# Two late weight transfers of a mixture-of-experts layer, each cut into 112, 8 and 8 partitions

## The chip, the cores and the metric

The kernel runs on one core of one Trainium2 chip. The metric is the device time of one execution in microseconds (us); shorter is better. The profile comes from one further execution that the hardware profiler recorded. PE is TensorE, ACT is ScalarE, DVE is VectorE, POOL is GpSimd, and SP is SyncE, which here only issues DMAs. SP's own instructions are marked SPq, and PE's weight loads PEld.

## What is computed

One layer of a decoder with 256 tokens of width 1024: two attention mixers, then a sparse feed-forward part with 32 experts of which each token takes four, then a norm. All the time this document speaks of lies in the experts:

```python
def moe_ffn(x, w_router, b_router, w_gate_up, b_gate_up, w_down, b_down):
    ...
    def expert_step(acc, params):
        wgu, bgu, wd, bd, g = params
        hgu = xt @ wgu + bgu
        gate = jnp.minimum(hgu[:, :D_EXPERT], SWIGLU_LIMIT)
        up = jnp.clip(hgu[:, D_EXPERT:], -SWIGLU_LIMIT, SWIGLU_LIMIT)
        y = ((up + 1.0) * (gate * jax.nn.sigmoid(SWIGLU_ALPHA * gate))) @ wd + bd
        return acc + g[:, None].astype(y.dtype) * y, None
    ...
return rmsnorm(h, norm_final_g)
```

Per expert the float32 weights are 8 MB for gate and up and 4 MB for down, 12 MB in all, and 32 experts make 384 MB that have to come in from memory.

## The kernel before

Each expert's weights come through a ring of ten slots in the on-chip memory, `ring`, each slot 128 partitions by 16 KB, so 2 MB. Four slots (0 to 3, or 4 to 7, in turn) hold an expert's gate and up weights, and slots 8 and 9 (`DN0` and `DN0 + 1`) hold the two halves of its down weights. SP issues every weight transfer, in one queue, in an order written out by hand (`experts` in the sync block). Before each transfer it waits on a counter of PE (`gu_used` or `dn_used`) that tells that the slot is free. Each slot has a semaphore (`slot_in`) that a transfer raises by 16 when all of it has landed, and PE waits on that before it reads the slot.

The experts are numbered 0 to 31 (`E - 1` is the last). PE works one expert apart: while it multiplies the gate and up weights of expert g (`gate_up`, line 1893), it does the down product of expert g - 1 (`down_rows`, line 1933). Between them it transposes the hidden values (`hidden_columns`, lines 1921 to 1925), which ACT copies back (line 913) as the left operand of the down product.

The end is written out by itself. SP issues, as the last of its queue: the second half of the down weights of expert 30 into slot 9 (line 534, through line 437), then `last_down`: the first half of the down weights of expert 31 into slot 0 (line 480), which has long been used, and the second half into slot 1 as one transfer of 1 MB (line 481) and two of 512 KB (line 484). After them comes the row of final gains (`gfin`, line 546). PE's `last_expert` waits for slot 9 at line 1999, does three of its four parts, transposes the hidden values of expert 31, and does the fourth part (line 2002). Then `last_down` waits for the copy by ACT (line 1960) and for slot 0 (line 1961), and does the last down product out of slots 0 and 1. `last_scatters` adds the result to the output banks, and DVE and ACT do the final norm.

A transfer of one slot, and PE's wait for it, are these lines:

```python
def load_dn(e, q):
    sp.dma_start(ring[:, DN0 + q, :], rows_of(dn, e, q)).then_inc(slot_in[DN0 + q], 16)
...
def down_rows(s, place, js, ready, uses, columns=hT, to=6):
    pe.wait_ge(ready, uses * 16)
```

Each of the 128 partitions of such a transfer takes one row of 16 KB that lies in one piece in memory. The program has a second copy of the expert code for further passes over more tokens (`more_passes`); it is branched over here.

Of the kernel before, what the change touches and what calls it, by code (L numbers as in the profile page):

```python
# [46 lines left out]
def hybrid_layer(nc, x, norm_mix_g, w_in, w_proj_sb, w_proj_moba, w_out, rel_bias, norm_ffn_g,  # L47
# [10 lines left out]
    E = w_router.shape[2]  # L58
# [4 lines left out]
    DN = 2  # L63
    DN0 = 2 * GU
    RING = DN0 + DN
    SLOT = 4 * D
    TURN = 6
    MIXED = 3
    CH = 512
    NCH = w_in.shape[2] // CH  # L70
    TRI = 3 * P
    assert NT == 2 and KD == 8 and HSB == 8 and HMB == 8 and NCH == 10 and E == 32 and CH == HALF

# [21 lines left out]
    with ctx:  # L95
        def sb(name, shape, dt=F32):
            return ctx.enter_context(nc.sbuf_tensor(name, shape, dt))

        def sem(name):
            return ctx.enter_context(nc.semaphore(name))  # L100
# [8 lines left out]
        ring = sb("ring", [P, RING, SLOT])  # L109
# [20 lines left out]
        neg_tri = sb("neg_tri", [P, P])  # L130
        neg_one = ring[:, 5, 7 * CH:7 * CH + P]
        before = sb("before", [P, P], BF16)
# [27 lines left out]
        gatesT = gates[:, :, :].rearrange("p t d -> p (t d)").rearrange("p (g n) -> p g n", n=T)  # L160
        gate_t = gates[:, 0, 0:CH]
        sig_t = gates[:, 0, CH:2 * CH]
        up_t = gates[:, 0, 2 * CH:3 * CH]
        h_t = gates[:, 0, 3 * CH:4 * CH]
# [10 lines left out]
        hT_last = gate_t.rearrange("p (c s) -> p c s", c=4)  # L175
# [95 lines left out]
        merged_rd = sem("merged_rd")  # L271
        slot_in = [sem(f"slot_in{s}") for s in range(RING)]
        half_in = sem("half_in")
        half_used = sem("half_used")
        spare_in = sem("spare_in")
        extra_in = sem("extra_in")
        gfin_in = sem("gfin_in")
        last_in = [sem(f"last_in{q}") for q in range(4)]
# [62 lines left out]
        dn_used = sem("dn_used")  # L341
# [39 lines left out]
        def _(sp):  # L381
# [42 lines left out]
            dn = w_down[0].rearrange("e (s p r) n -> e s p (r n)", p=P, r=4)  # L424

            def rows_of(src, e, q):
                return src[e, q] if isinstance(e, int) else src[bass.ds(e, 1), q].rearrange("o p n -> p (o n)")
# [8 lines left out]
            def load_dn(e, q):  # L436
                sp.dma_start(ring[:, DN0 + q, :], rows_of(dn, e, q)).then_inc(slot_in[DN0 + q], 16)
# [34 lines left out]
            def load_down(e, done, qs=range(DN)):  # L472
                for q in qs:
                    sp.wait_ge(dn_used, (e + done) * DN + (q + 1 - DN))
                    load_dn(e, q)

            def last_down(done):

                sp.wait_ge(gu_used, (E - 2 + done) * GU + DN)
                sp.dma_start(ring[:, 0, :], dn[E - 1, 0]).then_inc(last_in[0], 16)  # L480
                sp.dma_start(ring[:, 1, 0:2 * D], dn[E - 1, 1][:, 0:2 * D]).then_inc(last_in[1], 16)
                sp.wait_ge(gu_used, (E - 2 + done) * GU + DN + 1)
                for j in (2, 3):
                    sp.dma_start(ring[:, 1, j * D:(j + 1) * D], dn[E - 1, 1][:, j * D:(j + 1) * D]).then_inc(last_in[j], 16)

            def experts(done):
                if isinstance(done, int):
                    sp.wait_ge(start_rd, 2 * NT)
                    sp.dma_start(down_one[0], dn[1, 0][:, 0:2 * D]).then_inc(spare_in, 16)
                    sp.wait_ge(half_used, 1)  # L490
                    sp.dma_start(ring[:, 0, 0:2 * D], rows_of(gu, 2, 0)[:, 0:2 * D]).then_inc(half_in, 16)
                    sp.wait_ge(gu_used, 1)
                    sp.dma_start(ring[:, 0, 2 * D:4 * D], rows_of(gu, 2, 0)[:, 2 * D:4 * D]).then_inc(slot_in[0], 16)
                    load_gate_up(2, 0, done, range(1, GU))
                    load_gate_up(3, GU, done)
                    load_down(1, done, range(1, DN))
                    sp.wait_ge(dn_used, 1)
                    load_dn(2, 0)
                else:
                    load_gate_up(2, 0, done)  # L500
                    load_gate_up(3, GU, done)
                    load_down(1, done)
                load_gate_up(4, 0, done)
                load_down(2, done, range(1, DN) if isinstance(done, int) else range(DN))
                load_gate_up(5, GU, done)
                load_down(3, done)
                load_gate_up(6, 0, done)
                load_down(4, done)
                with sp.Fori(2, TURN) as i:
                    load_gate_up_wide(i * 2 + 3, GU, done)  # L510
                    load_down(i * 2 + 1, done)
                    load_gate_up_wide(i * 2 + 4, 0, done)
                    load_down(i * 2 + 2, done)
                with sp.Fori(TURN, TURN + MIXED) as i:
                    load_gate_up_wide(i * 2 + 3, GU, done, range(0, 1))
                    load_down(i * 2 + 1, done)
                    load_gate_up_wide(i * 2 + 3, GU, done, range(1, 2))
                    load_gate_up_wide(i * 2 + 4, 0, done, range(0, 1))
                    load_down(i * 2 + 2, done)
                    load_gate_up_wide(i * 2 + 4, 0, done, range(1, 2))  # L520
                with sp.Fori(TURN + MIXED, E // 2 - 3) as i:
                    load_down(i * 2 + 1, done)
                    load_gate_up_wide(i * 2 + 3, GU, done)
                    load_down(i * 2 + 2, done)
                    load_gate_up_wide(i * 2 + 4, 0, done)
                load_down(E - 5, done)
                load_gate_up(E - 3, GU, done)
                load_down(E - 4, done)
                load_gate_up(E - 2, 0, done)
                load_down(E - 3, done)  # L530
                load_gate_up(E - 1, GU, done, range(0, 2))
                load_down(E - 2, done, range(0, 1))
                load_gate_up(E - 1, GU, done, range(2, GU))
                load_down(E - 2, done, range(1, DN))
                last_down(done)

            def another_pass(r):
# [970 lines left out]
        def _(pe):  # L1508
# [418 lines left out]
            def down_rows(s, place, js, ready, uses, columns=hT, to=6):  # L1927
                pe.wait_ge(ready, uses * 16)
                for j in js:
                    k = 4 * s + j  # L1930
                    rows = columns[:, j, SLOTS * s:SLOTS * s + SLOTS]
                    for c in range(2):
                        ins = mm(bank[to][SLOTS * c:SLOTS * (c + 1), :], rows,  # L1933
                                 ring[:, place, j * D + c * CH:j * D + (c + 1) * CH], start=k == 0, stop=k == KD - 1)
                return ins
# [22 lines left out]

            def last_down(g, uses):
                pe.wait_ge(hT_rd, g + 1)  # L1960
                down_rows(0, 0, range(4), last_in[0], uses, hT_last, 5).then_inc(dn_used, 1)
                down_rows(1, 1, range(0, 2), last_in[1], uses, hT_last, 5)
                down_rows(1, 1, range(2, 3), last_in[2], uses, hT_last, 5)
                down_rows(1, 1, range(3, 4), last_in[3], uses, hT_last, 5).then_inc(dn_used, 1)
# [19 lines left out]
                else:  # L1984
                    down(g - 1, dn_uses, fewer=fewer)

            def last_expert(g, gu_uses, dn_uses, odd):

                gate_up(g, (0, 1), GU, gu_uses, odd)
                scatter_rows(g - 2)  # L1990
                weight_columns(g - 1)
                gate_up(g, (2, 3), GU, gu_uses, odd)
                pe.wait_ge(gT_rd, g)
                hidden_columns(g - 1)
                pe.wait_ge(y_rd, g - 1)
                down(g - 1, dn_uses, range(0, 1))
                gate_up(g, (4, 5, 6, 7), GU, gu_uses, odd)
                weight_columns(g)
                down_rows(1, DN0 + 1, range(0, 3), slot_in[DN0 + 1], dn_uses)
                pe.wait_ge(gT_rd, g + 1)  # L2000
                hidden_columns(g)
                down_rows(1, DN0 + 1, range(3, 4), slot_in[DN0 + 1], dn_uses).then_inc(dn_used, 1)
# [7 lines left out]
            def experts(done, r):  # L2010
                passes = 0 if r is None else r
                gu_before, dn_before = passes * (E // 2), passes * (E - 1)
# [35 lines left out]
                    expert(i * 2 + (done + 2), True, True, 0, i + (gu_before + 2), i * 2 + (dn_before + 2))  # L2048
                expert(done + (E - 3), True, True, GU, gu_before + E // 2 - 1, dn_before + (E - 3), 5 * passes + 4)
                expert(done + (E - 2), True, True, 0, gu_before + E // 2, dn_before + (E - 2), 5 * passes + 5)  # L2050
                last_expert(done + (E - 1), gu_before + E // 2, dn_before + (E - 1), 5 * passes + 5)
                last_down(done + (E - 1), passes + 1)
                last_scatters(done + (E - 1))

# [23 lines left out]
```

## Time and profile before

| what | us |
|---|---|
| median of 3 runs | 1134.36 (1134.32 to 1134.42) |
| profiled execution, its own time | 1135.26 |
| its span, first to last instruction | 1133.5 |
| PE busy | 1073.5 (95% of the span) |
| DVE, ACT, POOL busy | 260.1, 151.2, 122.1 |
| moved by DMA | 437.30 MB, mean 386 GB/s |

The span is what the profile shows in detail; 1135.26 less 1133.5, so 1.76 us, lies around it. "Idle before" an instruction is the time in which its engine did nothing, with what ended it. The DMA share of a stretch is the mean busy share of the core's 16 DMA engines. A matmul with float32 operands stands in the trace as two records; their durations overlap, so a group's start and total are used here, not its sum.

### The profile page before, as it was taken

Reading aid. Unit: us, or ns where it says so; the run is one execution under the profiler, and the core shown is the slowest. Engines: PE = TensorE matmul, PEld = TensorE weight load, DVE = VectorE, ACT = ScalarE, POOL = GpSimd, SP = SyncE. Lnnn points to the kernel's source line nnn. Section 1 sums busy time; section 2 is a strip of 40 time slices with the busy share of each in tenths; the row PEclk is TensorE's granted clock in tenths of the full one; section 3 lists DMA queues with packets and bytes.
Section 4 is the critical chain, followed back from the end, with each engine's and each line's share of the span. In section 5 each row is a group of like instructions: output and inputs, shape, how many; then the busy total and the mean of one; then the engine's idle time right before and its main releaser. Section 6 shows DMA issues by size and latency. Waiting matters only on the chain.

```text
span 1133.5 us, 14439 instructions
## 1 busy us (share of the span) xinstructions
PE 1073.5 (95%) x6022; PEld 452.1 (40%) x6022; DVE 260.1 (23%) x482; ACT 151.2 (13%) x315; POOL 122.1 (11%) x140
## 2 busy tenths in 40 slices
PE   8999999999999999999999999999999999999986
PEld 7676444533334333333333333333333333333322
DVE  2346756621111122111111122111210101111112
ACT  2233222420000010000000010000000000001002
POOL 1357592400000000000000000000000000000000
PEclk9999999999999999999999999999999999999999
DMA  9943238899999999999999999999999999999995
GB/s 326 350 175 149 95 137 352 348 379 426 430 427 432 430 426 430 431 428 430 431 429 436 429 434 430 430 430 432 430 429 435 429 429 431 431 427 427 427 427 227
DMA packets 36273, 437.30 MB, mean 386 GB/s; under 512 B 4440, under 2 KB 5520, under 8 KB 16944
## 3 DMA queue, kind: packets, MB, share of 16 engines
q1 hardware_dynamic: 34320, 435.44, 91.3%
q10 hardware_dynamic: 1920, 1.39, 0.5%
q8 instruction: 24, 0.39, 0.1%
q14 instruction: 9, 0.07, 0.0%
HBM read 435.76 MB, written 1.06 MB: 385 GB/s over the span
## 4 chain that ended last, share of the span: by engine, by line
PE 58%; DMA 38%; DVE 2%; issue 1%; ACT 0%; SPq 0%; POOL 0%; POOLq 0%
DMA ring<-in_w_down_dram 27%; PE bank L1893 20%; PE bank L1933 13%; DMA ring<-in_w_gate_up_dram 11%; PE bank L1572 9%; PE bank L1556 5%; PE bank L1868 3%; PE bank L1861 2%; PE bank L1924 1%; PE bank L1656 1%; PE bank L1881 1%; PE bank L1918 0%; PE bank L1681 0%; PE bank L1516 0%; PE bank L2007 0%
## 5 line engine op out<-in xcount | busy, mean ns | idle before, releaser
L1893 PE MATMUL bank<-ring,gates 128*64 128x512 f32 x2048 | 472.9, 604 | 16.8 <-DMA ring<-in_w_gate_up_dram 16.7
L1933 PE MATMUL bank<-ring,gates 128*64 128x512 f32 x1008 | 225.2, 594 | 27.8 <-DMA ring<-in_w_down_dram 27.0
L1893 PEld LDWEIGHTS bank<-ring,gates 128*64 128x64 f32 x2048 | 139.2, 138 | 262.9 <-issue 231.2
L1404 DVE TENSOR_SCALAR gates<-bank 128x512 f32<-128x512 f32 x31 | 21.4, 692 | 714.1 <-PE bank L1893 714.1
L1933 PEld LDWEIGHTS bank<-ring,gates 128*64 128x64 f32 x1008 | 71.7, 137 | 175.8 <-issue 139.4
L698 POOL COPY expert_sel<-expert_row 96x64 bf16 x32 | 7.5, 234 | 843.5 <-PE bank L1861 837.9
L608 POOL TENSOR_TENSOR ring<-ring 128x512 f32<-128x512 f32 x60 | 82.4, 1408 | 66.7 <-DVE ring L1061 34.6
L1861 PEld LDWEIGHTS bank<-onehot,qkT 128*128 128x128 bf16 x1488 | 52.1, 118 | 25.2 <-issue 25.2
L1868 PE MATMUL bank<-gates,scatter_w 64*128 64x512 f32 x248 | 61.8, 615 | 0.0
L918 ACT ACTIVATE gates<-gates 128x512 f32<-128x512 f32 x32 | 20.2, 630 | 284.2 <-DVE gates L1404 284.0
L1861 PE MATMUL bank<-onehot,qkT 128*128 128x64 bf16 x1488 | 55.5, 198 | 0.0
L1572 PE MATMUL bank<-ring 128*128 128x512 f32 x112 | 51.0, 597 | 1.1 <-DVE gates L1098 1.0
L922 ACT ACTIVATE gates<-bank 128x512 f32<-128x512 f32 x32 | 19.1, 597 | 203.0 <-PE bank L1933 203.0
L1572 PE MATMUL bank<-ring,extra 128*128 128x512 f32 x96 | 42.7, 595 | 0.0
L1868 PEld LDWEIGHTS bank<-gates,scatter_w 64*128 64x128 f32 x248 | 21.3, 186 | 39.8 <-issue 39.8
L913 ACT ACTIVATE gates<-bank 128x512 f32<-128x512 f32 x32 | 19.1, 597 | 120.4 <-PE bank L1924 120.4
L907 ACT ACTIVATE stat<-stat 128x1 f32<-128x1 f32 x32 | 6.5, 202 | 197.6 <-PE bank L1918 197.6
L1572 PEld LDWEIGHTS bank<-ring 128*128 128x128 f32 x112 | 20.7, 190 | 26.4 <-issue 23.0
L1556 PE MATMUL bank<-qkT,ring 128*128 128x256 f32 x128 | 29.0, 387 | 0.0
L1556 PE MATMUL bank<-ring 128*128 128x256 f32 x128 | 28.4, 381 | 0.0
L1924 PEld LDWEIGHTS bank<-ident,gates 128*128 128x128 f32 x128 | 17.9, 209 | 26.0 <-issue 26.0
L1572 PEld LDWEIGHTS bank<-ring,extra 128*128 128x128 f32 x96 | 18.0, 190 | 22.5 <-issue 22.5
(257 smaller groups left out, 646.9 us busy)
## 6 DMA issues: line engine op xcount, KB each, us to landing
ring<-in_w_gate_up_dram SPq DMA_DIRECT2D x44, 4096.0 KB, 28.1
ring<-in_w_down_dram SPq DMA_DIRECT2D x62, 2048.0 KB, 21.1
ring<-in_w_gate_up_dram SPq DMA_DIRECT2D x39, 2048.0 KB, 14.2
ring<-in_w_in_dram SPq DMA_DIRECT2D x9, 2048.0 KB, 15.2
ring<-in_w_out_dram SPq DMA_DIRECT2D x2, 2048.0 KB, 8.7
ring<-in_w_in_dram SPq DMA_DIRECT2D x4, 512.0 KB, 7.1
ring<-in_w_proj_sb_dram SPq DMA_DIRECT2D x1, 2048.0 KB, 7.7
ring<-in_w_proj_moba_dram SPq DMA_DIRECT2D x1, 2048.0 KB, 12.6
```

The costliest lines, as they stand in the source:

```text
L608: ins = nc.gpsimd.tensor_tensor(to[:, k, :], x[:, k, :], y[:, k, :], ALU.subtract)
L913: nc.scalar.activation(to[:, :, :], bank[7][:, :].rearrange("p (c s) -> p c s", c=4), ACT.Copy).then_inc(hT_rd, 1)
L918: nc.scalar.activation(sig_t, gate_t, ACT.Sigmoid, scale=SWIGLU_ALPHA).then_inc(sig_rd, 1)
L922: nc.scalar.activation(to, bank[at][:, :], ACT.Copy).then_inc(y_rd, 1)
L1404: V.tensor_scalar(gate_t, bank[4][:, :], SWIGLU_LIMIT, None, ALU.min).then_inc(gate_rd, 1)
L1556: ins = mm(bank[(u + (u >= KD)) % 2][:, 0:T], w[:, k, j * P:(j + 1) * P], cols[:, k, :], start=k == 0, stop=k == KD - 1)
L1572: ins = mm(bank[at][:, :], a[:, t, :], b[:, t, :], start=fresh and t == 0, stop=t == n - 1, skip_group_check=not fresh)
L1861: ins = mm(bank[7][:, k * SLOTS:(k + 1) * SLOTS], pieces[i][:, t, 4 * P * (k // 4) + k % 4:4 * P * (k // 4 + 1):4], onehot[:, t, :], start ...
L1868: ins = mm(bank[2 * t + c][:, :], weights[r, t, :], y[r, :], start=False, stop=True, skip_group_check=True)
L1893: ins = mm(bank[4 + i][SLOTS * c:SLOTS * (c + 1), :], xe[:, k, :], ring[:, base + k // 2, n0:n0 + CH], start=False, stop=k == KD - 1)
L1924: ins = tp(bank[7][:, c * P:(c + 1) * P], h_t[:, c::4], ident[:, :])
L1933: ins = mm(bank[to][SLOTS * c:SLOTS * (c + 1), :], rows, ring[:, place, j * D + c * CH:j * D + (c + 1) * CH], start=k == 0, stop=k == KD - 1)
```

## The change

Two transfers of 128 partitions, the second half of expert 30's down weights (slot 9) and the first half of expert 31's (slot 0), are each issued as three: partitions 0 to 111, 112 to 119, and 120 to 127. They stand at the same places of SP's queue, in this order. For slot 9 the first piece raises `slot_in[9]` and the two small ones a new semaphore `rest_in`; PE waits for both. For slot 0 all three raise `last_in[0]`, and PE waits for 48 instead of 16. The wait of SP ahead of slot 9 is the one that `load_down` had. Nothing else is different: the same bytes go to the same places, and PE's matmuls are the same.

```diff
+    BANDS = ((0, 112), (112, 120), (120, 128))
...
+        rest_in = sem("rest_in")
...
                 sp.wait_ge(gu_used, (E - 2 + done) * GU + DN)
-                sp.dma_start(ring[:, 0, :], dn[E - 1, 0]).then_inc(last_in[0], 16)
+                for a, b in BANDS:
+                    sp.dma_start(ring[a:b, 0, :], dn[E - 1, 0][a:b]).then_inc(last_in[0], 16)
...
-                load_down(E - 2, done, range(1, DN))
+                sp.wait_ge(dn_used, (E - 2 + done) * DN)
+                for n, (a, b) in enumerate(BANDS):
+                    sp.dma_start(ring[a:b, DN0 + 1, :], dn[E - 2, 1][a:b]).then_inc(slot_in[DN0 + 1] if n == 0 else rest_in, 16)
...
-                down_rows(0, 0, range(4), last_in[0], uses, hT_last, 5).then_inc(dn_used, 1)
+                down_rows(0, 0, range(4), last_in[0], len(BANDS) * uses, hT_last, 5).then_inc(dn_used, 1)
...
-                down_rows(1, DN0 + 1, range(0, 3), slot_in[DN0 + 1], dn_uses)
+                pe.wait_ge(slot_in[DN0 + 1], dn_uses * 16)
+                down_rows(1, DN0 + 1, range(0, 3), rest_in, (len(BANDS) - 1) * uses)
```

## Rows read from the trace of the kernel before

**Rows 1.** The page's part 4: the chain that ended last, shares by engine.

```profile
PE 58%; DMA 38%; DVE 2%; issue 1%; ACT 0%; SPq 0%; POOL 0%; POOLq 0%
```

**Rows 2.** The same chain in order of time, its end: start us, us, what.

```profile
1084.39 30.19 DMA ring<-in_w_down_dram
...
1114.71 7.09 PE bank L1933 x32
1121.80 3.66 PE bank L1868 x16
```

**Rows 3.** Timeline of PE: start us, us, operation, [idle before, what ended it].

```profile
1109.69 2.79 PE L1933 MATMUL bank<-ring,gates 128*64 128x512 f32 x12 [0.87 <-DMA ring<-in_w_down_dram]
1112.42 0.75 PE L1924 MATMUL bank<-ident,gates 128*128 128x128 f32 x4
1113.10 1.08 PE L1933 MATMUL bank<-ring,gates 128*64 128x512 f32 x4
1114.71 7.09 PE L1933 MATMUL bank<-ring,gates 128*64 128x512 f32 x32 [0.53 <-DMA ring<-in_w_down_dram]
```

**Rows 4.** Timeline of DVE and ACT in the same stretch.

```profile
1110.61 0.69 DVE L1414 SCALAR_TENSOR_TENSOR gates<-gates 128x512 f32<-128x512 f32 x1
...
1113.21 0.60 ACT L913 ACTIVATE gates<-bank 128x512 f32<-128x512 f32 x1 [2.99 <-PE bank L1924]
```

**Rows 5.** Timeline of SP's issues near the end: start us, us, line.

```profile
1084.02 0.33 SPq L437 DMA_DIRECT2D ring<-in_w_down_dram  x1
1084.39 0.43 SPq L480 DMA_DIRECT2D ring<-in_w_down_dram  x1
...
1092.73 0.34 SPq L546 DMA_DIRECT2D ring<-in_norm_final_g_dram  x1
```

**Rows 6.** Line 397, the store of an 8-partition tile: how long its issue took (ns).

```profile
L397 SPq DMA_DIRECT2D u_scratch<-ring x1: 3602/3602/3602, 30.4 to 30.4; - x1
```

**Rows 7.** DMA issues from 1060 us on: KB each, median us from issue to landing.

```profile
ring<-in_w_down_dram SPq DMA_DIRECT2D x1, 1024.0 KB, 32.2
ring<-in_w_down_dram SPq DMA_DIRECT2D x2, 512.0 KB, 33.3
...
ring<-in_norm_final_g_dram SPq DMA_DIRECT2D x1, 512.0 KB, 28.0
```

**Rows 8.** Windows at the end: stretch, us, busy times, clock, DMA share, GB/s.

```profile
1115.00:1116.00 1.00, 1.00 (x6) 0.34 (x4) 0.00 (x0) 0.00 (x0) 0.00 (x0) 1.00 1.00 397
1116.00:1117.00 1.00, 1.00 (x8) 0.46 (x6) 0.00 (x0) 0.00 (x0) 0.00 (x0) 1.00 0.80 324
1117.00:1118.00 1.00, 1.00 (x8) 0.40 (x6) 0.00 (x0) 0.00 (x0) 0.00 (x0) 1.00 0.58 238
1118.00:1119.00 1.00, 1.00 (x6) 0.34 (x4) 0.00 (x0) 0.00 (x0) 0.00 (x0) 1.00 0.49 201
1119.00:1120.00 1.00, 1.00 (x8) 0.46 (x6) 0.00 (x0) 0.00 (x0) 0.00 (x0) 1.00 0.28 115
1120.00:1121.00 1.00, 1.00 (x8) 0.40 (x6) 0.00 (x0) 0.00 (x0) 0.00 (x0) 1.00 0.03 12
```

**Rows 9.** Windows in three stretches with full queues.

```profile
16.50:20.50 4.00, 4.00 (x20) 3.04 (x18) 2.84 (x3) 0.00 (x0) 0.00 (x0) 1.00 1.01 235
30.00:42.00 12.00, 12.00 (x55) 9.11 (x54) 6.63 (x7) 2.15 (x3) 3.05 (x3) 1.00 1.05 386
1041.00:1108.00 67.00, 61.03 (x360) 22.05 (x356) 9.11 (x17) 4.60 (x10) 0.47 (x2) 1.00 1.01 428
```

**Rows 10.** Line 743, three loads of 256 KB into 32 partitions each: issues, then landing.

```profile
L743 ACTq DMA_DIRECT2D gates<-in_b_gate_up_dram x3: 318/440/442, 12.5 to 13.3; - x3
...
DMA to landing us min/median/max: 6.2/7.1/7.9
```

**Rows 11.** Windows around a stretch in which PE waited: busy PE first, clock third last.

```profile
853.10:856.54 3.44, 0.92 (x6) 0.35 (x8) 0.00 (x0) 0.00 (x0) 0.00 (x0) 1.00 1.04 448
856.55:859.95 3.40, 3.40 (x12) 0.96 (x10) 0.00 (x0) 0.00 (x0) 0.00 (x0) 0.50 0.92 395
```

More of the change, by code:

```diff
@@ L1985, in expert, with last_expert @@
                     down(g - 1, dn_uses, fewer=fewer)
-            def last_expert(g, gu_uses, dn_uses, odd):
+            def last_expert(g, gu_uses, dn_uses, odd, uses):
                 gate_up(g, (0, 1), GU, gu_uses, odd)
@@ L2050, in experts @@
                 expert(done + (E - 2), True, True, 0, gu_before + E // 2, dn_before + (E - 2), 5 * passes + 5)
-                last_expert(done + (E - 1), gu_before + E // 2, dn_before + (E - 1), 5 * passes + 5)
+                last_expert(done + (E - 1), gu_before + E // 2, dn_before + (E - 1), 5 * passes + 5, passes + 1)
                 last_down(done + (E - 1), passes + 1)
```

## The prediction

> **What bounds the kernel now.** I read the chain that ended last first, by engine and then in order of time. PE has 58% of it and DMA 38% [rows 1], and its last links are a down transfer that took 30.19 us from issue to landing, PE's last 32 matmul records, and 16 more that add the result [rows 2]. So at the end the kernel waits for weights, and after 1114.71 us it is PE without a gap. Next I read PE's timeline there. Two of its pauses end with the two transfers that the change cuts: 0.87 us before 1109.69 (slot 9, expert 30) and 0.53 us before 1114.71 (slot 0, expert 31) [rows 3]. Nothing else of the change is waited for. The issue of slot 0's transfer is at 1084.39, 30 us before its data is there [rows 2, 5], so the queue is deep and SP's issuing is not what is late.
>
> Third, the DMA side. Between 1041 and 1108 us the engines are busy all the time and move 428 GB/s [rows 9], 26.8 GB/s for each of 16. One row of 16 KB then takes an engine 16384 / 26.8e9 = 0.61 us, and a slot (128 rows, 8 for each engine) 4.9 us. At the end the engines do not finish together: the busy share is 1.00, 0.80, 0.58, 0.49, 0.28, 0.03 in the six microseconds from 1115 [rows 8]. About half are through by 1118.1, where the share stands near one half; the other half run on to 1120.73, where the last transfer in the queue lands (1092.73 + 28.0) [rows 5, 7]. So one half is ahead of the other by 1120.73 - 1118.1 = 2.6 us, a little over four rows. A transfer is complete when the last engine is, so the late half sets both of PE's pauses. No view names the engines.
>
> **The change part by part.** *What it can give.* 112 rows are 7 for each of 16 engines. If each piece of 8 rows goes to 8 engines of the early half, one row each, a cut transfer has 9 rows for these and 7 for the late ones. The late half gains 0.61 us per cut transfer, 1.22 us after two, and the early half, 2.6 us ahead, loses as much and is still in time. Whether pieces of 8 rows are placed so, the rows do not show.
>
> The Trainium skill ("DMA: Bandwidth & Descriptors", "Why a DMA increments its semaphore by 16 and not by 1") says that a transfer runs on the largest number of engines up to 16 that divides its row count, and that a DMA issued from SP takes the lowest-numbered ones. By that a piece of 8 rows always sits on the same 8 engines; whether those are the early half is not in the rows.
>
> *What a piece costs.* The trace has one case of much data into few partitions: the three loads of line 743, 256 KB each into 32 partitions. The first landed at 12.5 + 6.2 = 18.7 us and the third at 13.3 + 7.9 = 21.2 [rows 10], so the second and third took 2.5 us for 512 KB, 210 GB/s or 6.6 GB/s per partition. In that stretch the engines were as busy as ever (share 1.01) and yet moved 235 GB/s in all; a little later it was 386 at share 1.05 [rows 9]. Two queues shared the engines there, which may be part of it, but the nearest reading is that a partition group takes no more than this. At 6.6 GB/s a piece of 8 partitions takes 8 x 16384 / 52.5e9 = 2.5 us, in place of 0.61. Lower bound: 0.31 us, its bytes spread over all engines. Upper: 4.9 us, all 8 rows on one engine. I take 2.5, from the only row with a narrow destination.
>
> The Trainium skill ("SBUF — State Buffer", "Door 1: The DMA port swizzle") speaks against the change in the same way: the bandwidth depends on how many of 16 ports the partitions reach, and four adjacent partitions share one at about 27 GB/s. By that a piece of 8 adjacent partitions reaches two ports and takes an estimated 131072 / 54.4e9 = 2.4 us, and the sum below would come out 0.4 us lower. The 210 GB/s into 32 partitions agrees with its 189 to 218 for that width.
>
> *Sum of the pieces.* The engines that take the pieces need 7 x 0.61 + 2 x 2.5 = 9.3 us per cut transfer instead of 4.9, so 4.4 more. If they are the early half, slot 9 is complete 4.4 - 2.6 = 1.8 us later and slot 0 2 x 4.4 - 2.6 = 6.2 us later. The 112-partition pieces I take at 7 x 0.61; should they be placed less evenly over partitions than 128 rows are, they cost up to 1 us each more, and a staggered arrival of the engines takes up to 1 us off.
>
> *PE.* Slot 9 moves from 1109.69 to 1111.5, the fourth part of it ends near 1116.0 instead of 1114.18 [rows 3]. Slot 0 is there at 1114.6 + 6.2 = 1120.8; this swallows the first delay. The rest is 7.09 + 3.66 us of PE and then the norm, unchanged [rows 2]. The later quarters come 32.2 and 33.3 us after their issues now, at about 1117.1 and up to 1119.5, with PE needing them from 1118.4 on [rows 3, 7]; they shift with the queue by the same 6.2 us, so their slack of over a microsecond stays. The gains row likewise.
>
> *PE's clock.* From 1116.0 to 1120.8 PE would be idle for 4.8 us. Where PE was busy for only 0.92 of 3.44 us, the granted clock of the next 3.40 us was 0.50, the lower of the two levels, 1.2 GHz [rows 11]. Such a stretch costs between nothing (it falls into the idle time) and 3.4 / 2 = 1.7 us. I take the middle, 0.9 us.
>
> *Issuing.* Four more issues on SP: 0.33 to 0.43 us each, 1.6 us in all [rows 5]. The one 8-partition transfer in the trace took 3.6 us to issue [rows 6]; with that it is 14 us. Behind them in the queue are the quarters of slot 1 and the gains, issued at 1084.9 to 1092.7 and landing 28 to 33 us later [rows 5, 7], so either is covered; without the cover it would be as many microseconds. PE gets one more wait, between 0 and 0.1 us, on a path where the data is later anyway: nothing.
>
> Together 6.2 + 0.9 = 7.1 us. On the profiled execution's own 1135.26 that gives 1142.4. The median of the runs is 0.9 us below that execution, so I forecast 1141.5 us. Its own range is 1138.5 (2.0 us for a piece, no clock stretch) to 1143.5 (full clock stretch, uneven 112-row pieces).
>
> **Rivals.** *The halves are evened out.* The pieces cost only their bytes and go to the early engines. Slot 9 lands 0.61 us earlier and PE starts it at 1109.08. Its three parts end at 1111.87, after the DVE result at 1111.30 that the transposes need [rows 3, 4]; so ACT's copy, and the fourth part, come 0.61 us earlier, the latter ending at 1113.57. Slot 0 lands at 1114.58 - 1.22 = 1113.36, so PE goes on at once, 1.1 us before 1114.71, and nothing later gives way: 1133.3 us, not slower, and by 0.10% only. It takes over from the forecast where a piece takes less than about 1.0 us: 2 x (7 x 0.61 + 2 x 1.0 - 4.9) = 2.7 us, so the early half is then only as late as the late half is today. For it: the late engines are seen, and the numbers fit four rows. Against it: the 235 GB/s.
>
> *The wrong half.* Pieces at byte cost, but on the late engines: slot 0 is 1.22 us later, and PE with it: 1135.6 us, 0.11%. Nothing in the rows speaks for or against.
>
> *It does nothing.* The pieces are spread over all 16 engines, half a row each: 1134.4 us.
>
> *One engine each.* All 8 rows on one engine: 2 x 2 x 4.9 us of extra rows, over 1150 us.
>
> **How the numbers follow.** Forecast 0.62, evened out 0.25, wrong half 0.06, nothing 0.03, one engine or another slowing 0.03, a larger gain 0.01. A measurement of this kernel tells about 0.2%, 2.3 us, from no change. Evened out, wrong half and nothing all lie within it: 0.34. Faster 0.01, slower 0.65. The range has to hold 8 in 10, and the forecast's own range is not enough, so it reaches down to the evened case, 1133.0, and up to 1143.5.
>
> **What would show it.** In the profile after: PE's idle time before line 1933's last 32 records, 0.53 us now, grows to about 5 us and ends with a down DMA; the records themselves still take 7.09 us, or up to 8.8 with the clock row at 0.50. In the windows from 1110 us on the DMA share stays near 1.00 while the rate falls clearly below 428 GB/s, as in the stretch of line 743. If instead the share falls from 1.00 to zero within about a microsecond near 1119.5 and both pauses are gone, the pieces cost their bytes and my price of 2.5 us is wrong. If the share keeps its step at one half, but it ends later, they went to the wrong half.

## The result, and the profile after

| what | before | after |
|---|---|---|
| median, us | 1134.39 (4 runs) | 1152.72 (1150.57 to 1153.85, 4 runs) |
| ratio | | 1.0158, interval 1.0145 to 1.017 |
| profiled execution, its own time | 1135.26 | 1150.57 |
| its span | 1133.5 | 1148.8 |

The change makes the kernel 18.3 us slower by the medians. That is the forecast's direction, but far beyond its 7.1 us and its range. The profiled execution is the quickest of the four after; it is 1150.57 - 1135.26 = 15.3 us over the one before, and the steps below are about these 15.3. No profile of a slower execution exists, so the other 3 us have no rows; on record is only the mean granted clock of the other three, 0.984 to 0.986 where the profiled one has 0.990, and whether that is the 3 us is not shown.

The chain that ended last, in order of time (start us, us, what), answers to [rows 2]. Every line number above the change is 5 higher: 1933 is now 1938, 1893 is 1898.

```profile
1085.50 43.37 DMA ring<-in_w_down_dram
...
1129.01 8.52 PE bank L1938 x32
1137.53 3.66 PE bank L1873 x16
```

The same three links, but the transfer takes 43.37 us from issue to landing instead of 30.19, and PE's last product 8.52 instead of 7.09. PE's timeline (start us, us, operation, idle before and what ended it) shows where it begins; it answers to [rows 3].

```profile
1108.39 5.16 PE L1898 MATMUL bank<-ring,gates 128*64 128x512 f32 x16 [5.15 <-DMA ring<-in_w_gate_up_dram]
...
1118.39 4.42 PE L1938 MATMUL bank<-ring,gates 128*64 128x512 f32 x12 [4.48 <-DMA ring<-in_w_down_dram]
...
1129.01 8.52 PE L1938 MATMUL bank<-ring,gates 128*64 128x512 f32 x32 [4.51 <-DMA ring<-in_w_down_dram]
```

In the kernel before, the first of these is this row:

```profile
1104.80 3.65 PE L1893 MATMUL bank<-ring,gates 128*64 128x512 f32 x16 [1.24 <-DMA ring<-in_w_gate_up_dram]
```

So the last gate and up transfer, which is whole and stands ahead of the cut ones, already lands 3.6 us later. Slot 9 follows 8.7 us later than before (1118.39 against 1109.69 [rows 3]) and slot 0 14.3 us later (1129.01 against 1114.71). The steps are 3.6, 5.1 and 5.6 us. The last product adds 8.52 - 7.09 = 1.4, and 15.7 us are there when it ends; the rest of the kernel gives 0.4 back.

The windows (stretch, us, busy times, then clock, DMA share, GB/s last) answer to [rows 9]; the first three are single microseconds:

```profile
1099.00:1100.00 1.00, 0.91 (x6) 0.20 (x4) 0.00 (x0) 0.00 (x0) 0.00 (x0) 1.00 1.00 426
1100.00:1101.00 1.00, 1.00 (x8) 0.37 (x6) 0.00 (x0) 0.00 (x0) 0.00 (x0) 1.00 1.30 360
1101.00:1102.00 1.00, 1.00 (x8) 0.35 (x6) 0.00 (x0) 0.00 (x0) 0.00 (x0) 1.00 1.02 213
...
1100.00:1104.00 4.00, 3.24 (x16) 0.86 (x12) 0.00 (x0) 0.00 (x0) 0.00 (x0) 1.00 1.17 254
1104.00:1108.00 4.00, 0.00 (x0) 0.00 (x0) 0.00 (x0) 0.00 (x0) 0.00 (x0) 1.00 0.91 201
1108.00:1112.00 4.00, 3.61 (x10) 1.15 (x12) 0.00 (x0) 0.00 (x0) 0.00 (x0) 0.57 1.00 213
...
1124.00:1128.00 4.00, 0.50 (x4) 0.00 (x0) 0.00 (x0) 0.72 (x2) 0.00 (x0) 1.00 0.99 259
...
1129.01:1137.50 8.49, 8.49 (x34) 2.85 (x34) 0.00 (x0) 0.00 (x0) 0.00 (x0) 0.83 0.27 110
```

The engines are as busy as ever and move half as much: 201 to 259 GB/s where [rows 9] had 428. At a share of 1.00 and 213 GB/s a row of 16 KB takes an engine 16384 x 16 / 213e9 = 1.23 us instead of 0.61. The half rate lasts from about 1101 to 1127 us. The two cut transfers alone, 4 MB, would be 20 us of it at 206 GB/s, and 26 us at 213 GB/s are 5.5 MB, so bytes of whole transfers moved at half rate too. It begins 7 us before the gate and up transfer is read (1108.39) and almost 4 us before that was read in the kernel before (1104.80): a cut transfer is already being moved while the whole one ahead of it is still on its way. The last row is the stretch of PE's last product, at a mean granted clock of 0.83.

Issuing is not what is late. SP's three issues take 1.05 us for slot 9 and 1.02 for slot 0, where one took 0.33 and 0.43 [rows 5], and the transfers behind them are still issued 30 us and more before they land:

```profile
1083.69 1.05 SPq L539 DMA_DIRECT2D ring<-in_w_down_dram  x3
1084.78 1.02 SPq L483 DMA_DIRECT2D ring<-in_w_down_dram  x3
```

### The profile page after: what moved, and what is told of

It is laid out like the page before. It is cut to its first block, busy times and chain, and to the rows that moved or that the text cites. A ratio compares the mean times of both kernels' runs of the same rounds, so it can differ in the third digit from the quotient of the medians.

```text
span 1148.8 us, 14444 instructions
## 1 busy us (share of the span) xinstructions
PE 1076.2 (94%) x6022; PEld 452.1 (39%) x6022; DVE 259.9 (23%) x482; ACT 151.2 (13%) x315; POOL 122.3 (11%) x140
## 4 chain that ended last, share of the span: by engine, by line
PE 56%; DMA 41%; DVE 1%; SPq 1%; issue 1%; ACT 0%; POOL 0%; POOLq 0%
DMA ring<-in_w_down_dram 30%; PE bank L1898 19%; PE bank L1938 13%; DMA ring<-in_w_gate_up_dram 11%; PE bank L1577 10%; PE bank L1561 5%; PE bank L1873 2%; PE bank L1866 2%; PE bank L1929 1%; DMA ring<-in_w_in_dram 1%; PE bank L1661 1%; PE bank L1886 0%; PE bank L1923 0%; PE bank L1686 0%; PE bank L2013 0%
```

## The experiments

Three explanations stood after the result: the narrow pieces of 8 partitions cost (N); the piece of 112 partitions is dealt out unevenly and costs more than its 4.3 us (P); or the number of transfers costs. Runs of the kernel before beside these runs had medians of 1134.5 to 1134.8.

### A list of prices

Behind the kernel's output, SP issues six transfers of a kind, waits for all, and goes on to the next kind. The time of the run includes the list.

```diff
+            for n in range(6):
+                sp.dma_start(ring[0:112, n, :], dn[n, 0][0:112]).then_inc(price[1], 16)
+            sp.wait_ge(price[1], 16 + 16 * 6)
...
```

> The kernel before, with a price list behind its last output: nine stages, each begun when the one before has landed, each of six transfers of 16 KB rows into six slots: 128 partitions, 112, 8 adjacent (112 to 119), 8 that stand 12 apart (0, 12, ... 84), 16 (112 to 127), 64 (0 to 63), 96, 120, and last six times the changed kernel's three pieces. The added stages are extra work after the result and lengthen the run. Theory N (narrow pieces: a group of adjacent partitions takes data no faster than one engine brings it): per transfer 128: 4.9 us, 112: 4.3, 8 adjacent: 2.4 to 2.5, 8 apart: 0.6, 16: 2.4, 64: 4.9, and the three pieces 8 to 9.3. Theory P (the 112-partition piece is dealt to the engines so that several write the same partitions' group at once): 112: clearly over 4.3, some 5 to 8 us, and likewise 96 and 120. Theory E (only the number of rows per engine counts): 8 adjacent and 8 apart both 0.6, 16: 0.6, 64: 2.4, 112: 4.3, three pieces 5.5.

SP's timeline of this run: each row is the first issue of a kind. The next row's start less this one's is what six of them took.

```profile
1132.01 3.13 SPq L555 DMA_DIRECT2D ring<-in_w_down_dram  x6
1164.19 3.08 SPq L558 DMA_DIRECT2D ring<-in_w_down_dram  x6
1209.08 1.99 SPq L561 DMA_DIRECT2D ring<-in_w_down_dram  x6
1225.29 4.13 SPq L564 DMA_DIRECT2D ring<-in_w_down_dram  x6
1232.69 2.64 SPq L567 DMA_DIRECT2D ring<-in_w_down_dram  x6
1249.05 3.75 SPq L570 DMA_DIRECT2D ring<-in_w_down_dram  x6
1282.04 2.81 SPq L573 DMA_DIRECT2D ring<-in_w_down_dram  x6
1325.02 2.99 SPq L576 DMA_DIRECT2D ring<-in_w_down_dram  x6
1385.75 6.42 SPq L580 DMA_DIRECT2D ring<-in_w_down_dram  x18
```

Six whole transfers took 1164.19 - 1132.01 = 32.2 us. With 4.9 us each, an estimated 2.8 us remain for the way there and back, once per kind; I take them off everywhere.

| partitions of one transfer | six, less 2.8, by six: us | rows of 16 KB |
|---|---|---|
| 0 to 127 (L555) | 4.9 | 128 |
| 0 to 111 (L558) | 7.0 | 112 |
| 112 to 119 (L561) | 2.2 | 8 |
| 8, standing 12 apart (L564) | 0.8 | 8 |
| 112 to 127 (L567) | 2.3 | 16 |
| 0 to 63 (L570) | 5.0 | 64 |
| 0 to 95 (L573) | 6.7 | 96 |
| 0 to 119 (L576) | 9.7 | 120 |
| 0 to 111, 112 to 119, 120 to 127 (L580, to the span's end at 1449.3) | 10.1 | 128 |

Three of its windows, in the stretches of L555, L558 and L570 (DMA share and GB/s last):

```profile
1136.00:1160.00 24.00, 0.00 (x0) 0.00 (x0) 0.00 (x0) 0.00 (x0) 0.00 (x0) 0.50 1.00 429
1167.00:1205.00 38.00, 0.00 (x0) 0.00 (x0) 0.00 (x0) 0.00 (x0) 0.00 (x0) 0.50 1.01 263
...
1252.00:1280.00 28.00, 0.00 (x0) 0.00 (x0) 0.00 (x0) 0.00 (x0) 0.00 (x0) 0.50 1.01 206
```

Both N and P hold, and E falls. A piece of 8 adjacent partitions costs 2.2 us and 8 rows standing apart at most 0.8 (SP issued these one each 0.69 us, 4.13 for six, so their own price may be lower): it is where the rows lie and not their number. The 112 rows cost more than all 128. And 64 adjacent partitions keep all engines busy (1.01) at half the rate. Everything the change sends, sent alone, is 10.1 us per cut transfer instead of 4.9: 2 x 5.2 = 10.4 us.

### One cut at a time

Slot 9 alone is cut, or slot 0 alone; the diffs are the halves of the change.

> Only the transfer into slot 9 is cut in three, slot 0's is whole as before. In the changed kernel slot 9's data came 8.6 us later than before and slot 0's 14.3 us. If each cut costs on its own (N or P): slot 9 about 8 us later as in the changed kernel, slot 0 some 6 to 8 us later, the run 1141 to 1144 us. If the loss comes only from two cuts behind each other: about 1136 us.

> Only the transfer into slot 0 is cut in three, slot 9's is whole. If a cut transfer also slows what is ahead of it in the queue (engines of the early half write into the partitions of engines that are behind): slot 9, which is not cut, comes 1 to 4 us later too, slot 0 some 6 to 8 us later, the run 1140 to 1144 us. If it only slows itself: slot 9 within 0.3 us of 1109.7, slot 0 6 to 8 us later.

Measured 1145.2 (two runs; ratio 1.0088, interval 1.0058 to 1.0117) and 1146.0 (1143.05 to 1148.37; 1.0103, 1.0082 to 1.0123). Both medians lie above the 1144 us at which the expectations ended. The profiled execution of the second is its quickest, 1143.05. PE's timeline of the run with slot 9 alone:

```profile
1107.77 5.01 PE L1897 MATMUL bank<-ring,gates 128*64 128x512 f32 x16 [4.35 <-DMA ring<-in_w_gate_up_dram]
...
1119.06 5.33 PE L1937 MATMUL bank<-ring,gates 128*64 128x512 f32 x12 [5.91 <-DMA ring<-in_w_down_dram]
```

and with slot 0 alone:

```profile
1104.97 3.65 PE L1895 MATMUL bank<-ring,gates 128*64 128x512 f32 x16 [1.25 <-DMA ring<-in_w_gate_up_dram]
...
1113.66 5.21 PE L1935 MATMUL bank<-ring,gates 128*64 128x512 f32 x12 [4.67 <-DMA ring<-in_w_down_dram]
...
1123.70 7.09 PE L1935 MATMUL bank<-ring,gates 128*64 128x512 f32 x32 [3.14 <-DMA ring<-in_w_down_dram]
```

In each, the transfer directly ahead of the cut one is late though it is whole: the gate and up transfer by 3.0 us in the first, slot 9 by 4.0 (1113.66 against 1109.69) in the second, where the gate and up transfer, two places ahead, lands as before. Then the cut one adds its own 6.4 and 5.0 us. So one cut costs about 4 + 5, and two in a row 4 + 5 + 5: the neighbour ahead is paid once. That is why each alone has well over half of the loss.

### Three transfers along the row

```diff
+    BANDS = ((0, 3584), (3584, 3840), (3840, 4096))
...
+                for a, b in BANDS:
+                    sp.dma_start(ring[:, 0, a:b], dn[E - 1, 0][:, a:b]).then_inc(last_in[0], 16)
```

> Both transfers are issued as three, as in the change, but all three go over all 128 partitions and the cut is along the row: 14 KB, 1 KB and 1 KB of each. The number of issues, of semaphore raises and waits is the changed kernel's. If the number of transfers is the cause (theory C): some 1140 to 1153 us. If the partitions are (N or P): 1134.4 to 1135.5 us, the short rows costing a few tenths.

Measured 1134.94 (8 runs; 1.0004, 0.9993 to 1.0015). Six transfers instead of two, with the bytes in the same shares, each over all partitions, cost nothing. The number of transfers, SP's issues and PE's extra wait are out.

### Extra pieces

Both transfers stay whole, and four pieces of 8 partitions of data that nobody reads are added, two ahead of slot 0's transfer and two behind it; once as adjacent partitions, once as every fourth of partitions 96 to 127.

```diff
+                for rows in (slice(112, 120), slice(120, 128)):
+                    sp.dma_start(ring[rows, 3, :], dn[E - 1, 1][rows]).then_inc(rest_in, 16)
```

> The kernel before, its transfers into slots 9 and 0 whole, with four extra loads of 8 rows of 16 KB into a slot that is free by then: partitions 112 to 119 and 120 to 127 ahead of slot 0's transfer, 96 to 103 and 104 to 111 behind it. They are extra work that nobody reads; by their bytes alone they put 0.61 us each on the eight engines that carry them. Theory N (a piece of 8 adjacent partitions takes 2.4 us also in the middle of the queue): slot 0's data 2 to 5 us later, the run 1136.5 to 1140 us. If a piece is cheap in the queue (the 112-row pieces are then the whole loss): 1134.4 to 1135.8 us.

> As the run before, but the same 32 partitions (96 to 127) are loaded in four extra pieces of 8 partitions that stand 4 apart. Bytes, rows, engines and number of issues are the same. Theory N: the pieces' partitions lie in eight groups instead of two, a piece takes 0.7 us, and the run is 1134.4 to 1136 us; with the price of 0.7 us on the early half there is nothing to see, on the late half slot 0 is 1.4 us later. If what costs is that 8 engines carry a piece while the others go on, it is as slow as the run before.

Measured 1146.08 (1.0099, 1.008 to 1.0117) and 1142.68 (1.0069, 1.005 to 1.0087), two runs each. Both expectations were missed: the adjacent pieces were to cost 2 to 5 us at slot 0 and cost 9.2. PE's timeline with the adjacent ones:

```profile
1114.59 4.49 PE L1940 MATMUL bank<-ring,gates 128*64 128x512 f32 x12 [5.53 <-DMA ring<-in_w_down_dram]
...
1123.86 8.78 PE L1940 MATMUL bank<-ring,gates 128*64 128x512 f32 x32 [3.10 <-DMA ring<-in_w_down_dram]
```

That is about the price of four pieces, and it falls on the transfer ahead of them: slot 9, ahead of the first two, is read 4.9 us later, for two pieces of 2.2, and slot 0, ahead of the other two, another 4.3. The pieces that stand apart should have been nearly free, and are not:

```profile
1113.03 5.38 PE L1940 MATMUL bank<-ring,gates 128*64 128x512 f32 x12 [3.93 <-DMA ring<-in_w_down_dram]
...
1121.30 3.65 PE L1940 MATMUL bank<-ring,gates 128*64 128x512 f32 x16 [1.19 <-DMA ring<-in_w_down_dram]
```

Slot 9 comes 3.3 us later and slot 0 6.6. My expectation had left out which partitions the pieces stand in; the second list, below, prices that.

### The lead of one half, used

If the late engines are what counts, giving the last quarter of slot 9 to the early ones should gain, if pieces of 8 rows go to these. 12 KB of each row go as one whole transfer, and the last 4 KB in sixteen pieces of 8 partitions that stand 4 apart.

```diff
+                for block in range(0, P, 32):
+                    for r in range(4):
+                        rows = slice(block + r, block + 32, 4)
+                        sp.dma_start(ring[rows, DN0 + 1, 3 * D:4 * D], dn[E - 2, 1][rows, 3 * D:4 * D]).then_inc(rest_in, 16)
```

> The aim of the change without narrow pieces: slot 9's transfer is cut along the row into the first 12 KB over all 128 partitions and the last 4 KB in sixteen pieces of 8 partitions that stand 4 apart. The eight engines of the pieces carry two rows more than the others, as after both cuts of the change; slot 0 is whole. Theory evened out (an engine's rows are all that counts, the pieces go to the early half): slots 9 and 0 each 1.2 us earlier, the run 1133.1 us. Theory port (a partition group takes no more than one engine brings, so the late engines' partitions fill no faster whoever writes them): no gain, 1134.3 to 1137 us. Wrong half: 1135.6 us or more.

Measured 1140.46 (4 runs; 1.0047, 1.0032 to 1.0062): slower. Slot 9 is read at 1114.25, 4.6 us later. The rival of the prediction by which the halves are evened out falls in this form too, in which no piece has adjacent partitions; of the three theories only "wrong half", 1135.6 us or more, leaves room for the time. How much of the 4.6 us is the count of pieces and how much their place, this run does not tell.

### A second list: whose partitions

Five of each kind, the same manner; "whole +" is a whole transfer and then the piece.

```diff
+            for n in range(5):
+                sp.dma_start(ring[:, n, :], dn[n, 0]).then_inc(price[0], 16)
+                sp.dma_start(ring[0:32:4, n + 5, :], dn[n, 1][0:32:4]).then_inc(price[0], 16)
+            sp.wait_ge(price[0], 16 + 16 * 10)
...
+                sp.dma_start(ring[0:128:2, n + 5, :], dn[n, 1][0:128:2]).then_inc(price[5], 16)
```

> A second list of prices, added behind the output, so the whole run is some 250 us longer. Five of each, between waits, all rows of 16 KB: (1) a whole transfer and a piece of 8 partitions standing 4 apart in 0 to 31; (2) the same with the piece in 64 to 95; (3) the same with the piece in 96 to 127; (4) a whole transfer and a piece of 8 adjacent ones, 0 to 7; (5) the same with 112 to 119; (6) 64 partitions, every other one of all 128; (7) the upper 64, 64 to 127; (8) a whole transfer and then one of 112; (9) 12 KB of every partition in one transfer and the last 4 KB in sixteen pieces of 8 partitions 4 apart. Theory G (each of 16 groups of partitions takes data at one engine's rate; a transfer is slow where several engines meet on one group, and then also the transfer that runs beside it): (1) is the cheapest, 4.9 + 0.6 to 0.7 = about 5.6 us, and (2) and (3) cost the same or, where the piece's engines meet the owners of these groups, 0.6 us or more above (1); (4) and (5) cost 4.9 + 2.4 = 7.3 or more; (6) lies below the 5.05 of the lower 64, down to 2.5, since its rows lie in all 16 groups; (7) is 5.05 as the lower 64; (8) is above 4.9 + 7.0 = 11.9; (9) is above 6.5. Rival Q (an engine is slowed only by its own queue, and a transfer lands with its busiest engine): (1), (2), (3) 5.5, (4) and (5) 7.3, (6) 2.5, (8) 11.9 at most and (9) at most 3.7 + 2.6 = 6.3.

SP's timeline of this run, the first issue of each kind:

```profile
1132.74 0.34 SPq L555 DMA_DIRECT2D ring<-in_w_down_dram  x1
...
1163.10 0.33 SPq L559 DMA_DIRECT2D ring<-in_w_down_dram  x1
...
1196.68 0.33 SPq L563 DMA_DIRECT2D ring<-in_w_down_dram  x1
...
1230.03 0.33 SPq L567 DMA_DIRECT2D ring<-in_w_down_dram  x1
...
1270.91 0.33 SPq L571 DMA_DIRECT2D ring<-in_w_down_dram  x1
...
1311.87 3.13 SPq L575 DMA_DIRECT2D ring<-in_w_down_dram  x5
1327.18 3.10 SPq L578 DMA_DIRECT2D ring<-in_w_down_dram  x5
1355.01 0.35 SPq L581 DMA_DIRECT2D ring<-in_w_down_dram  x1
...
1416.94 0.33 SPq L585 DMA_DIRECT2D ring<-in_w_down_dram  x1
```

| kind | five, less 2.8, by five: us |
|---|---|
| whole + 8 in 0 to 31, 4 apart (L555) | 5.5 |
| whole + 8 in 64 to 95, 4 apart (L559) | 6.2 |
| whole + 8 in 96 to 127, 4 apart (L563) | 6.1 |
| whole + 0 to 7 (L567) | 7.6 |
| whole + 112 to 119 (L571) | 7.6 |
| 64: every other one (L575) | 2.5 |
| 64: 64 to 127 (L578) | 5.0 |
| whole + 0 to 111 (L581) | 11.8 |

Two of its windows, every other partition and then the upper 64:

```profile
1314.00:1325.00 11.00, 0.00 (x0) 0.00 (x0) 0.00 (x0) 0.00 (x0) 0.00 (x0) 0.50 1.00 419
1330.00:1352.00 22.00, 0.00 (x0) 0.00 (x0) 0.00 (x0) 0.00 (x0) 0.00 (x0) 0.50 0.99 203
```

The same number of rows, and all engines busy in both (1.00 and 0.99): 419 GB/s when every other partition is taken and 203 when they are the upper half. And a piece that stands apart costs 0.6 us beside a whole transfer in partitions 0 to 31, but 1.2 to 1.3 in 64 to 127. Theory G had these two dearer and rival Q had not. But a whole transfer and one of 112, 11.8, came as Q had it: G had them above the sum of 4.9 and 7.0, since one should slow the other. With 8 adjacent partitions 7.6 is 0.5 over 4.9 + 2.2. By the price of 1.2 the four pieces that stood apart in the kernel cost 4 x 1.2 = 4.8 us of the 6.6 by which slot 0 came later; the rest was not settled. Of the sixteen pieces of 4 KB there is no price: SP issued them one each 0.66 us, 10.7 for sixteen, and was the bound of that kind.

The Trainium skill ("SBUF — State Buffer", "Door 1: The DMA port swizzle (why [64,N] ≈ [32,N])") puts partitions into 16 ports, 0 to 63 on eight of them and 64 to 127 on the other eight, with some 27 GB/s for each. The 206 and 203 GB/s agree, and the 419 for every other partition, which meets all 16. The Trainium skill ("DMA: Bandwidth & Descriptors", "The descriptor swizzle") says that in a whole transfer each engine writes into one port, the first eight engines those of partitions 0 to 63. That the pieces are dearer in 64 to 127 agrees with it, if they run on the first eight, as the Trainium skill says in the section that the prediction cites ("Why a DMA increments its semaphore by 16 and not by 1"); no view here names an engine.

### Cut in the kernel without narrow pieces, and with one

The two transfers as 64 and 64 partitions, and as 112 and 16:

```diff
+    BANDS = ((0, 64), (64, 128))
```

> The two transfers are each sent as two of 64 partitions, 0 to 63 and 64 to 127: both deal evenly over 16 engines (4 packets each), no piece is narrow, and two issues are saved against the change. Theory G (engines that meet on one group of partitions halve each other): each cut transfer takes 2 x 5.05 = 10.1 us, as the list of prices says of 64 partitions, instead of 4.9, so the end comes 10.4 us later, with the pauses' clock stretch of 1.4 us and up to 3 us of the transfers ahead 1144 to 1150; in the trace the DMA share stays near 1 while the rate is about 206 GB/s. Rival N (the narrow pieces of 8 partitions on 8 engines are the whole cost): no cost, 1134 to 1136.

> The two transfers are each sent as two, of 112 partitions and of the last 16 in one piece (16 engines, one packet each, instead of two pieces on 8 engines). Theory G: 16 adjacent partitions are few groups, so the piece costs what the list says, 2.4 us, as one piece of 8 does: each cut transfer 7.0 + 2.4 = 9.4 instead of 4.9, +9 us for two, with the clock stretch and the transfers ahead 1145 to 1151, some 2 to 5 us under the change. Rival E (too few engines: 8 of the 16 carry the small pieces): with all 16 engines on the 16 partitions the piece costs 0.6 to 1 us and the 112 take 4.3: 1134.4 to 1137.

Measured 1150.72 (4 runs; 1.0141, 1.0124 to 1.0158) and 1151.15 (4 runs; 1.0141, 1.0124 to 1.0158). Both are about as slow as the change, and just above the upper ends that theory G gave (1150 and 1151). So the narrow pieces are not needed for the loss, and sending the last 16 partitions as one piece does not help. The gate and up transfer ahead is late in both, first with 64 and 64, then with 112 and 16:

```profile
1109.93 5.97 PE L1898 MATMUL bank<-ring,gates 128*64 128x512 f32 x16 [6.56 <-DMA ring<-in_w_gate_up_dram]
```

```profile
1109.71 5.84 PE L1898 MATMUL bank<-ring,gates 128*64 128x512 f32 x16 [5.41 <-DMA ring<-in_w_gate_up_dram]
```

Two windows of the run with 64 and 64:

```profile
1104.00:1108.00 4.00, 0.00 (x0) 0.00 (x0) 0.00 (x0) 0.00 (x0) 0.00 (x0) 0.98 1.01 213
...
1116.00:1120.00 4.00, 1.31 (x8) 0.58 (x9) 2.63 (x4) 0.99 (x3) 0.00 (x0) 1.00 1.00 219
```

The picture is that of the change: all engines busy at half the rate.

### Even and odd partitions

```diff
+    BANDS = (slice(0, 128, 2), slice(1, 128, 2))
```

> The two transfers are each sent as two of 64 partitions again, but as the even and the odd ones instead of the lower and the upper half: the same bytes, the same count of transfers, packets and engines as in the run with 64 and 64, only the partitions that stand together differ. Theory G (what costs is where the rows of one transfer lie; 64 partitions cost about 2.5 us where every other one is taken and 5.0 where the lower or upper half is): 1134.4 to 1137, the DMA share and the rate as in the kernel before (some 400 GB/s between 1100 and 1112 us), and the last 32 records 7.09 us. Rival B (a cut across the partitions costs as such, because a queue of whole transfers is mixed with others): 1146 to 1152, as 64 and 64.

Measured 1134.6 (11 runs; 1.0001, 0.9992 to 1.001): no difference from the kernel before. PE's timeline and two windows of it:

```profile
1104.69 3.65 PE L1898 MATMUL bank<-ring,gates 128*64 128x512 f32 x16 [1.24 <-DMA ring<-in_w_gate_up_dram]
...
1114.58 7.09 PE L1938 MATMUL bank<-ring,gates 128*64 128x512 f32 x32 [0.41 <-DMA ring<-in_w_down_dram]
```

```profile
1104.00:1108.00 4.00, 3.31 (x16) 1.06 (x16) 0.00 (x0) 0.00 (x0) 0.00 (x0) 1.00 1.00 426
...
1112.00:1116.00 4.00, 3.58 (x20) 1.44 (x18) 0.00 (x0) 1.20 (x2) 0.00 (x0) 1.00 0.99 403
```

Against the run with 64 and 64, only the choice of rows for each transfer differs, and 16.1 us go away, the late gate and up transfer among them. What costs is which rows stand together in one transfer.

In all these runs a piece's rows lie in memory as they lie in the partitions, so no run parts the two, and that the rows' places in memory cost instead was not tested. Two rows speak for the partitions. A load of line 743 reads 256 KB that lie in one piece into 32 partitions, at 210 GB/s by [rows 10]. Sixteen adjacent partitions of the first list, 256 KB in one piece too, took 2.3 us, some 115 GB/s. That is an argument from two rows and not a test.

### Cut along the row, each part waited for when it is needed

Slot 9 as 12 and 4 KB of each row, slot 0 as 8 and 8 KB; PE starts on the first part of a slot before the second has landed.

```diff
+                sp.dma_start(ring[:, 0, 0:2 * D], dn[E - 1, 0][:, 0:2 * D]).then_inc(last_in[0], 16)
+                sp.dma_start(ring[:, 0, 2 * D:4 * D], dn[E - 1, 0][:, 2 * D:4 * D]).then_inc(half_in, 16)
...
-                down_rows(0, 0, range(4), last_in[0], uses, hT_last, 5).then_inc(dn_used, 1)
+                down_rows(0, 0, range(0, 2), last_in[0], uses, hT_last, 5)
+                down_rows(0, 0, range(2, 4), half_in, uses + 1, hT_last, 5).then_inc(dn_used, 1)
```

> Neither kernel: slots 9 and 0 are cut along the row, over all 128 partitions (12 KB and 4 KB; 8 KB and 8 KB), and PE waits for each part only when it needs it. No engine's load changes. From the rows of before: slot 9's first part lands 1.2 us earlier, so PE's pause of 0.87 us there goes; slot 0's first half lands 2.4 us earlier, so the pause of 0.53 us goes too, and PE's last product starts 1.3 us earlier, with the last quarters' slack nearly used up. Expected 1133.1 us, 0.12% less; if the last quarters come too late for it, 1133.1 to 1134.4. If the number of transfers cost something: above 1134.5.

Measured 1134.2 (11 runs) against 1134.8 (15 runs); 0.9991, interval 0.9982 to 1.0000. That is the fastest version seen, by 0.6 us of the 1.3 that I expected, at the edge of what can be told from no change. PE now does all of slot 0 without a pause and next waits 0.53 us for the first part of slot 1, until 1117.81; the stream of weights is again what it waits for:

```profile
1117.81 3.65 PE L1937 MATMUL bank<-ring,gates 128*64 128x512 f32 x16 [0.53 <-DMA ring<-in_w_down_dram]
```

## Why the prediction was right in direction and wrong in size

*What bounds the end.* Right: PE waits there for the two down transfers, and their lateness goes straight to the end.

*A piece of 8 partitions, 2.5 us.* Right in size: 2.2 in the list, and at most 0.8 when 8 rows stand apart. The price came from the three loads of line 743 [rows 10] and their 235 GB/s [rows 9]. The rule behind it, 6.6 GB/s for each partition, was lucky: the list gives 7.4 for 8 adjacent partitions, but 3.2 for 64 and 2.3 for 112, so it holds for narrow ranges only and says nothing of the 112.

*"The 112-partition pieces I take at 7 x 0.61."* Mis-sized: 7.0 us alone, not 4.3. The allowance, "up to 1 us each more", was too small too (2.7). The pieces of one cut transfer overlap, so that it takes 10.1 us and not 7.0 + 2 x 2.2; the term of 9.3 was 0.8 us short, 1.6 for two. I looked at the spread of rows over engines (16 divides 112) and not at the spread over partitions, and the run with 64 and 64 shows that this alone can halve the rate.

*"Slot 0 2 x 4.4 - 2.6 = 6.2 us later."* This is the step that failed, for slot 9 as well (8.7 us later, not 4.4 - 2.6 = 1.8). I let the engines that are ahead use up their lead of 2.6 us before anything is late. Measured, the transfer ahead of the first cut one is 3.6 us late instead. So the term was +3.6 and not -2.6, 6.2 us apart; with the 1.6 above that is 7.8 of the 8.1 us by which slot 0 came later than forecast (14.3 against 6.2). In the prediction's own terms: 3.6 + 2 x 5.2 = 14.0. The runs with one cut and those with 64 and 64 and 112 and 16 show this neighbour late as well, and even and odd partitions leave it in time. Only the extra adjacent pieces cost their list price and no more (9.2 us at slot 0 for 4 x 2.2 = 8.8), though half of it fell on the transfer ahead of them. The rate falls to half before the transfer ahead is in (from 426 GB/s at 1099 us to 213 at 1101), so the cut transfer is worked on beside it. My reading is that the engines that are ahead begin on the cut transfer, whose rows lie in partitions that other engines are still filling, and slow those. That is argued, not shown, since no view names an engine. The list does not bear it out: whole transfers and ones of 112 follow each other there five times and cost 11.8 = 4.9 + 7.0, with no extra; that queue begins empty, so a lead may be missing there. So why the transfer ahead pays some 4 us once is open. The lead was loosely read too: the shares of [rows 8] fall step by step from 1.00 to 0.03, with 0.58 and 0.49 on the way, so they fit engines that end one after another from 1116 to 1121 better than two halves 2.6 us apart.

*Clock.* Right in kind: after the pause of 4.51 us the records took 8.52 us at a mean granted clock of 0.83, 1.4 us more, inside the 0 to 1.7 of the prediction and above its 0.9.

*Issuing.* Right: six issues in 2.1 us, and nothing behind them waits.

*The rivals.* "Evened out" and "the wrong half" needed pieces at the cost of their bytes, "nothing" needed no cost at all; all fall with the result and the list. "One engine each" reached over 1150 us, as the kernel did, but a piece has half the cost it gave (2.2, not 4.9).

*What would show it.* The pause before the last 32 records was to grow to about 5 us, with the DMA share near 1 and a rate well below 428: both came (4.51; 201 to 259). I had looked for these at slot 0 only, not for the 5.15 us in front of the gate and up product.

## What to carry to other kernels

Cut a transfer along the row, or into even and odd partitions; a cut into ranges of adjacent partitions can halve the rate while the engines look fully busy, so read the GB/s beside the DMA share. Price a transfer by the partitions that it reaches, and sum the price over the transfers in flight around it, the one ahead included. Do not count a lead that some engines seem to have at a transfer's end as slack for what is queued next: here it was forecast at 2.6 us of slack, and the transfer ahead was 3.6 us late.

## What the runs showed of the hardware

- 112, 96 and 120 adjacent partitions took 7.0, 6.7 and 9.7 us where 128 took 4.9, with the same 16 KB per partition.
- 64 partitions took 5.0 us as 0 to 63 or 64 to 127 (206 and 203 GB/s) and 2.5 us as every other one (419), with the engines busy all the time in each.
- A transfer cut into ranges of adjacent partitions also slowed the whole transfer queued directly ahead of it, by 3.0 to 5.1 us in five kernels; in the one with slot 0 alone cut, the transfer two places ahead was in time.
